# A hybrid decoder layer on one core: the low parts of the weight panels made by VectorE instead of GpSimd

## The reference

```
xn = RMSNorm(h); [z | xBC | dt | q | k | v] = xn @ w_in
mix = concat(SSD_heads(z, xBC, dt), SWA_sink_heads(q, k, v)) @ w_out
h = h + mix
h = h + CrossAttn(RMSNorm(h), memory K/V)   (4 heads over 256 memory tokens)
h = h + SwiGLU(RMSNorm(h))                  (D_FF = 2816)
y = RMSNorm(h)
```

## Time and profile before

| | |
|---|---|
| median of 3 runs | 2900.93 us (2899.84 to 2901.79) |
| the profiled execution's own time | 2905.87 us |
| its span, first to last instruction | 2904.1 us |
| mean granted TensorE clock | 0.98 of full |
| PE busy | 2779.9 us (96%), 13539 matmuls |
| DVE busy | 1450.4 us (50%), 2193 instructions |
| ACT busy | 1167.3 us (40%) |
| POOL busy | 1008.2 us (35%), 451 instructions |

### The profile page before, as it was taken

One profiled execution on the slowest core, in us unless ns is written; L12 is line 12 of the kernel. 1 busy time (PEld: TensorE's weight loads), 2 busy tenths in 40 slices (PEclk: granted clock), 3 DMA queues, 4 the chain that ended last, 5 costly groups with the idle time before them and its releaser, 6 DMA issues. The chain is left out here.

```text
span 2904.1 us, 34707 instructions
## 1 busy us (share of the span) xinstructions
PE 2779.9 (96%) x13539; PEld 2244.9 (77%) x13539; DVE 1450.4 (50%) x2193; ACT 1167.3 (40%) x1878; POOL 1008.2 (35%) x451
## 2 busy tenths in 40 slices
PE   6799789999999999999999999999999987999998
PEld 3478667878778878888778878888778876888886
DVE  4446565556662284557652475556642444322224
ACT  3455644543452244443442345443542343322222
POOL 2122023433334443333334433433344432333331
PEclk9899989999999999999999999999999998999999
DMA  9653554222223353322223353222223341222221
GB/s 308 219 128 116 167 148 117 80 87 74 76 73 95 101 165 104 88 78 79 73 80 95 109 152 102 80 87 73 73 87 95 122 130 51 76 82 82 80 80 60
DMA packets 415094, 303.05 MB, mean 104 GB/s; under 512 B 48075, under 2 KB 384079, under 8 KB 413890
## 3 DMA queue, kind: packets, MB, share of 16 engines
q1 hardware_dynamic: 412474, 294.41, 33.9%
q10 hardware_dynamic: 1880, 6.34, 0.6%
q0 software_dynamic: 576, 0.07, 0.0%
HBM read 277.90 MB, written 23.85 MB: 104 GB/s over the span
## 5 line engine op out<-in xcount | busy, mean ns | idle before, releaser
L1634 POOL TENSOR_TENSOR w_lo<-w_raw,w_hi 128x1024 fp32r<-128x1024 f32 x398 | 976.2, 2455 | 1744.0 <-ACT w_hi L1648 1743.8
L1648 ACT ACTIVATE w_hi<-w_raw 128x1024 fp32r<-128x1024 f32 x398 | 419.2, 1054 | 552.2 <-PE G L2938 270.3
L2624 PE MATMUL L<-xa_h,w_hi 128*128 128x512 f32 x1184 | 475.1, 401 | 0.0
L2625 PE MATMUL L<-xa_h,w_lo 128*128 128x512 f32 x1184 | 464.4, 392 | 0.0
L2626 PE MATMUL L<-xa_l,w_hi 128*128 128x512 f32 x1184 | 464.4, 392 | 0.0
L2624 PEld LDWEIGHTS L<-xa_h,w_hi 128*128 128x128 f32 x1184 | 224.3, 189 | 54.1 <-issue 6.7
L2626 PEld LDWEIGHTS L<-xa_l,w_hi 128*128 128x128 f32 x1184 | 223.8, 189 | 48.0
L2625 PEld LDWEIGHTS L<-xa_h,w_lo 128*128 128x128 f32 x1184 | 224.3, 189 | 45.9 <-issue 1.0
L2624 PE MATMUL L<-xb_h,w_hi 128*128 128x512 f32 x576 | 231.2, 401 | 15.8 <-DVE xb_l L2055 15.8
L2626 PE MATMUL L<-xb_l,w_hi 128*128 128x512 f32 x576 | 225.5, 392 | 0.0
L2625 PE MATMUL L<-xb_h,w_lo 128*128 128x512 f32 x576 | 225.3, 391 | 0.0
(11 more groups left out here) (570 smaller groups left out, 4925.0 us busy)
## 6 DMA issues: line engine op xcount, KB each, us to landing
w_raw<-in_w_down_dram SPq DMA_DIRECT2D x88, 512.0 KB, 3.4
w_raw<-in_w_gate_dram SPq DMA_DIRECT2D x66, 512.0 KB, 3.8
w_raw<-in_w_up_dram SPq DMA_DIRECT2D x66, 512.0 KB, 3.8
w_raw<-in_w_in_dram SPq DMA_DIRECT2D x56, 512.0 KB, 3.8
xt<-xT_dram SPq DMA_DIRECT2D x56, 256.0 KB, 4.7
w_raw<-in_w_gate_dram SPq DMA_DIRECT2D x44, 256.0 KB, 2.8
w_raw<-in_w_up_dram SPq DMA_DIRECT2D x44, 256.0 KB, 3.1
fwin<-in_w_in_dram SPq DMA_DIRECT2D x8, 1156.0 KB, 10.3
```

Source lines behind the costliest of these rows:

```text
L1634: pool.tensor_tensor(w_lo[:, n % RING, 0:w], w_raw[:, n % RING, 0:w], w_hi[:, n % RING, 0:w].bitcast(F32), ALU.subtract)\
L1648: act.activation(w_hi[:, n % RING, 0:w], w_raw[:, n % RING, 0:w], ACT.Copy)\
L2624: pe.matmul(acc, wh, rh, start=(k == 0), stop=False)
L2625: pe.matmul(acc, wl, rh, start=False, stop=False)
```

## The change

GpSimd's loop over the panels is gone; it keeps the low parts of the first two panels and the two operations on the memory keys. VectorE gets `low_panel(n)`, which waits for ScalarE's `w_hi` of panel n and makes `w_lo`; it is called once for each panel, two panels ahead of the step in which it stands: at the start of the step in the in-projection, W, Q, E, the gate and up steps of F and every second output of O; behind the additions in the down steps; and at four places of the norm between O and F for the steps v and z.

```
-                for n in range(AHEAD, NPAN):
-                    if n == 13:
-                        pool.wait_ge(s["piece_ev"], piece_index[("K", CH - 1)] + 1)
-                        pool.tensor_copy(kmh0[:], kmT[:]).then_inc(s["km_hi"], 1)
-                        pool.wait_ge(s["km_hi"], 1)
-                        pool.tensor_tensor(kml0[:], kmT[:], kmh0[:].bitcast(F32), ALU.subtract).then_inc(s["km_lo"], 1)
-                    pool.wait_ge(s["hi_ready"], n + 1)
-                    w = panels[n][1] * panels[n][2] * P
-                    pool.tensor_tensor(w_lo[:, n % RING, 0:w], w_raw[:, n % RING, 0:w],
-                                       w_hi[:, n % RING, 0:w].bitcast(F32), ALU.subtract)\
-                        .then_inc(s["lo_ready"], 1)
...
             def _(dve):
+                def low_panel(n):
+                    if n >= NPAN:
+                        return
+                    dve.wait_ge(s["hi_ready"], n + 1)
+                    w = panels[n][1] * panels[n][2] * P
+                    dve.tensor_tensor(w_lo[:, n % RING, 0:w], w_raw[:, n % RING, 0:w],
+                                      w_hi[:, n % RING, 0:w].bitcast(F32), ALU.subtract).then_inc(s["lo_ready"], 1)
...
                 def in_slot(b, n, role):
+                    low_panel(n + AHEAD)
...
                     for n in range(KT):
+                        low_panel(pos[("W", b, n)] + AHEAD)
...
                     for n in range(KT):
+                        if n % 2 == 0:
+                            low_panel(pos[("O", b, n // 2)] + AHEAD)
...
                     sum_squares(b, 1, KT - 1)
+                    if more:
+                        low_panel(pos[("I", b + 1, ("v", 0))] + AHEAD)
...
                         kind, f, m = step
+                        if kind != "down":
+                            low_panel(pos[("F", b, step)] + AHEAD)
                         o0 = first_out[pos[("F", b, step)]]
                         if p == GATED_ROOT:
                             next(mix)
...
                                 if f == len(FG) - 1 and n >= 1:
                                     sum_squares(b, 2, n - 1)
+                            low_panel(pos[("F", b, step)] + AHEAD)
```

More of the change, by code:

```diff
@@ L1625, in _ @@
                                    pattern=[[1, P]], channel_multiplier=1).then_inc(s["consts"], 1)
-                for n in range(AHEAD, NPAN):
-                    if n == 13:
-                        pool.wait_ge(s["piece_ev"], piece_index[("K", CH - 1)] + 1)
-                        pool.tensor_copy(kmh0[:], kmT[:]).then_inc(s["km_hi"], 1)
-                        pool.wait_ge(s["km_hi"], 1)
-                        pool.tensor_tensor(kml0[:], kmT[:], kmh0[:].bitcast(F32), ALU.subtract).then_inc(s["km_lo"], 1)
-                    pool.wait_ge(s["hi_ready"], n + 1)
-                    w = panels[n][1] * panels[n][2] * P
-                    pool.tensor_tensor(w_lo[:, n % RING, 0:w], w_raw[:, n % RING, 0:w],
-                                       w_hi[:, n % RING, 0:w].bitcast(F32), ALU.subtract)\
-                        .then_inc(s["lo_ready"], 1)
+                pool.wait_ge(s["piece_ev"], piece_index[("K", CH - 1)] + 1)
+                pool.tensor_copy(kmh0[:], kmT[:]).then_inc(s["km_hi"], 1)
+                pool.wait_ge(s["km_hi"], 1)
+                pool.tensor_tensor(kml0[:], kmT[:], kmh0[:].bitcast(F32), ALU.subtract).then_inc(s["km_lo"], 1)
             @blk.scalar
@@ L2425, in last_ffn @@
                         o = out_of("E", b, step)
+                        low_panel(pos[("E", b, step)] + AHEAD)
                         if p in hidden_at:
@@ L2513, in _ @@
                     for n in range(CH):
+                        low_panel(pos[("Q", b, n)] + AHEAD)
                         o = out_of("Q", b, n)
@@ L2536, in _ @@
                     sum_squares(b, 1, KT - 1)
-                    if not more:
+                    if more:
+                        low_panel(pos[("I", b + 1, ("v", 0))] + AHEAD)
+                    else:
                         dve.tensor_tensor(fold[:], ident[:, 0:S], ident[:, S:P], ALU.add)
@@ L2542, in _ @@
                     diagonal(token_rsqrt(b, 1))
+                    if more:
+                        low_panel(pos[("I", b + 1, ("z", 1))] + AHEAD)
                     row_back(b, 1)
                     for i in range(KT):
+                        if more and i == 4:
+                            low_panel(pos[("I", b + 1, ("z", 2))] + AHEAD)
                         norm3_t(b, i)
@@ L2548, in _ @@
                     norm3_lo(b, KT - 1)
+                    if more:
+                        low_panel(pos[("I", b + 1, ("z", 3))] + AHEAD)
                     if not more:
```

## The result

| | before | changed |
|---|---|---|
| median | 2900.56 us (4 runs, 2899.84 to 2901.79) | 2879.60 us (4 runs, 2877.48 to 2882.87) |
| ratio, 95% interval | | 0.992 (0.9908 to 0.9933) |
| the profiled execution's span | 2904.1 us | 2881.1 us |

The changed kernel is 21 us (0.8%) faster. Run again with the experiments (five executions, 2878.88 us beside 2903.88 for the kernel before) it gave 0.9916 (0.9902 to 0.9929), 25 us.

A forecast was written before the change was run, and what follows sets the result against it. TensorE, busy 96% of the span, was taken as the bound. Terms of -3.1, -3.1, -2.5 and -0.9 summed to -9.6 us, giving 2891 us from a median of 2900.93; the range was 2884 to 2902.

The forecast's parts named there:

- The low part on VectorE costs 1.22 us, and nothing behind it: Each low part moved to VectorE was priced at 1.22 us, with bounds 1.14 and 2.4, and nothing added after it.
- The Trainium skill's flush: Rival: a drain after each VectorE operation lengthens the W turn to 5.97 us, 2908 us; longer-operation case, chance 0.03.
- VectorE is held by GpSimd, and the holds go: VectorE's operations wait while GpSimd works; 350 us of such holds were estimated to go, leaving VectorE near 55% busy.
- The gated root and the attention unit, -6.2: In F of three blocks, TensorE's waits for `zs` and `SC` go: -3.1 us at each of the two places.
- The root's margin: At the gated root, `zs` was to end 0.7 us before TensorE is free for it.
- The W stage, -2.5 us: Three W turns a block shorten from 5.30 to 5.02 us, 0.84 us a block, easing the k panel's wait.
- the ring: In W, a VectorE turn passes through ScalarE's rounding, 5.02 us; as a slower rival 6.30 us, 2915 us, chance 0.09.
- W catches up: Rival: VectorE follows TensorE in W and the k panel's waits go, -8.6 us instead of -2.5, 2885 us; chance 0.12.
- The norm behind O and the end of F, -0.9: At both places a `sqsum` loses its hold and a low part comes in: -0.9 us together, bounds +1.5 and -3.8.
- Placed at nothing: Gate and up steps, SyncE's loads, the last block's E stage and the memory-key operations were given no gain or loss.
- The slower rivals: VectorE waiting for ScalarE in W, 2915 us, 0.09; longer VectorE operations, 2914 us, 0.03; an unseen place, 0.02.
- The sum: All terms together: -9.6 us against the profiled execution's 2905.9 us, giving a forecast of 2891 us.

## Why the prediction was wrong, point by point

- *The low part on VectorE costs 1.22 us, and nothing behind it.* Right: 1.224 mean, and the next operation starts 1.14 after it. The Trainium skill's flush ("VectorE: DVE Perf Modes", "The DRAIN you can't avoid"), by which 2908 was estimated, is not seen here. The same section of the Trainium skill says that a next operation that is not held starts earlier, and this start, 0.08 us before the end, agrees with that, though no run shows which operations are held.
- *VectorE is held by GpSimd, and the holds go.* Right: `hid_l` 1.66 to 0.69 us, busy 54% (55 forecast; its terms add up to 1583 us, not 1590, and 1561.8 was measured). The two runs with idle work on GpSimd show that it is its reading; `tensor_scalar` operations are lengthened too, and there writes alone are enough.
- *The gated root and the attention unit, -6.2.* Right in place and mechanism, mis-sized a little: 7.5. Each wait of 1.02 to 1.06 us was 1.25 by the matmuls' starts. The root's margin was 0.3 us, not 0.7.
- *The W stage, -2.5 us.* This is the step that failed; it gave 11.5 in blocks 1 and 2 (5.6 and 5.9). The prediction took a hold away from the turn, gave it back as a ring, and so left the k panel's wait nearly as it was; the runs show that the wait closes, and that closing it is worth about twice its length. Three things are missing. First, the turn: I added up durations (5.02), but an operation on VectorE or ScalarE starts some 0.08 us before the row of the one ahead of it ends, and the ring measured 4.74; three turns give 1.7 instead of 0.84. Second, I counted the turns from the `xt` that waited for its transfer at 1065.45 as if that one stayed where it was. Before it lie two more holds of `sqsum` in the kernel before (2.67 us at 1055.72 and 2.28 us at 1062.72), and with them gone the last `xt` starts 2.2 us behind the k panel's first matmul (1070.55 - 1068.32), where it was 5.4 (1081.37 - 1075.94). That is 3.2 us for a wait of 2.69: the wait closes. The prediction's rival "W catches up", -8.6 in W and 2885 us, had this case, at 0.12, but priced the waits at their own length. Third, the clock: behind each wait of 2.5 to 2.7 us TensorE ran at the lower level for part of the following stretches, which the windows of the kernel before show and I had not read. With the waits it goes too: block 1's wait of 2.69 was worth 4.6 and block 2's of 2.45 was worth 5.9, and a wait of 2.63 put back by hand cost 6.1. So the waits' own 5.1 us are not half of the 11.5. Another 1.0 us of block 1 lies ahead of the k panel, 0.7 of it where TensorE had waited 0.33 us for GpSimd's low part itself (at 1064.50), which the prediction put at nothing.
- *The norm behind O and the end of F, -0.9.* Mis-sized: 0.9 to 0.6 a block at the norm and 0.25 a block at the end of F, 2.9 in all.
- *Placed at nothing.* The gate and up steps: right. For the down steps the text named the idle time of `sg`; there the cover is the order, as the run with the low part in front shows (18 us). The last block is open: between 2308 and 2461 both profiles of the changed kernel lose 2.0 us against the kernel before, but the two runs with a wait put back by hand, which have the same code there, lose 0.1.
- *The slower rivals.* The ring is real, but 0.7 us shorter than TensorE's panel. That a low part ahead of a product's evacuation can make TensorE wait is real as well, in F rather than in W, and only with the order that the change avoids.
- *The sum.* In the profiles 7.5 + 11.5 + 2.9 = 21.9 us stand against the 9.6 forecast; set-up and block 0 give another 3.0 and the last block takes 2.6, both of which differ between executions of the same code.

## What to carry to other kernels

An engine that TensorE hardly ever waits for can still cost time: if GpSimd reads the memory while VectorE runs two-input operations, look at VectorE's mean durations against the shortest of the same shape, and at what waits behind them. When work moves into another engine's in-order queue, check each place for what stands behind it: the same operation, ahead of or behind two additions, was 18 us apart here. And price a wait of TensorE by its own length and by the granted clock in the stretches behind it; here a wait of 2.45 to 3.07 us cost 1.7 to 2.4 times its length.

## What was not expected of the hardware

- What a wait of TensorE costs beyond itself is not set by its length. At the k panel of blocks 1 and 2, waits of 3.07, 2.63, 2.72 and 2.45 us cost 3.4 to 3.5 more each, two of 2.69 us 1.9 and 1.8 more, one of 1.18 us 1.9 more and one of 1.58 us 0.2 more. Open.
- GpSimd's twelve fills per panel (0.30 us each, 47% of the span) left the means of VectorE's two-input operations unchanged to 1 ns and lengthened `tensor_scalar` on `zs` by 101 ns; four subtractions of 240 numbers took 0.87 us each and lengthened those of VectorE's operations with two inputs in the core's memory that they met by 0.3 to 0.4 us.
- Block 0's wait for `xb_l` differed between executions of the same code (3.0 and 2.3 us in two profiles of the changed kernel). With the set-up, which differed by up to 4 us between profiles, it limits what single executions can tell; the medians' intervals of about 0.13% are the measure.
